# Output projection 2 of a two-block transformer kernel as seven products of quadrants

## The chip, the cores and the metric

The kernel runs on one NeuronCore (1 of 8) of a Trainium2 chip, in one launch. The metric is device microseconds of that core. The kernel before has a median of 1051.36 us over 3 runs (1051.34 to 1053.21).

Engines by their names in the profile: PE is TensorE (PEld its weight loads), DVE is VectorE, ACT is ScalarE, POOL is GpSimd, SP is SyncE, which issues most transfers.

## The reference, cut to what matters

Two transformer blocks run one after the other on 512 rows (tokens) of 1024 features, in float32. The second block's end is

```python
m = sigmoid(g_a) * y_a + sigmoid(g_b) * y_b          # 512 x 1024
h = layer_norm(ALPHA * h + m @ w_out_2, ln1_g, ln1_b)  # output projection 2, w_out_2 is 1024 x 1024
f = square(relu(h @ w_ff1)) @ w_ff2                    # 1024 -> 4096 -> 1024
h = layer_norm(ALPHA * h + f, ln2_g, ln2_b)
```

The change touches `m @ w_out_2` and the first 512 columns of `h @ w_ff1`.

## The kernel before, in words

**Numbers in two halves.** TensorE multiplies rounded float32 values. To keep accuracy each operand is split: ScalarE copies it rounded (`hi`), VectorE subtracts that copy from the original (`lo`), and TensorE makes three matmuls for each product of tiles: hi x hi, hi x lo, lo x hi (`three`, L624 to L626). So each weight block (128 x 2048) costs ScalarE one rounding copy and VectorE one subtraction, and each activation operand as well. Helper `lower` (L1861) is the subtraction of all of them.

**Blocks in order.** `block_list` lists the weight blocks. SyncE loads block n into one of two raw tiles, after VectorE has finished the low half of block n - 2. The engines each walk the same list; all instructions are written out by hand in a fixed order for each engine, and each engine takes its own strictly in that order. Semaphores (`wait_ge`, `then_inc`) tie the engines.

**Around the change.** The last four blocks before output projection 2 are those of `g_b`: TensorE makes gates in banks 0 and 1, ScalarE applies the sigmoid in the bank, VectorE multiplies (`r_silu<-r_silu,bank`, L2645) and adds the two branches (`add_branches`, `r_silu<-r_silu,u_gelu`, L2392). Each addition raises `m_ready`; at 8 all of m is there, in tile R (`r_silu`).

**Output projection 2 before.** Four blocks of w_out_2 (two halves of the columns, two halves of the inner dimension), each against the matching half of m, split in `x_hi`, `x_lo`: 4 blocks x 4 row tiles x 4 chunks x 3 = 192 matmuls of 512 columns, in banks 2 to 5. The last two blocks are interleaved (`tm_pair`, L738), so that row tile 0 is done first and the layer norm starts before the projection ends. VectorE adds each bank to the residual (`add_half`, L2545: 8 instructions), takes row statistics (L2396, L2399), centres (L2572) and, once GpSimd has made the reciprocal root (L3004, L3005), scales (L2581). TensorE transposes the four rows of h (`turn_row`, L779, 8 transposes of 128 x 128 each): rows 0 and 1 inside the projection, rows 2 and 3 inside what follows. ScalarE copies the transposed row (`act_t_hi`), and VectorE makes its low half (`h1_rows_lo`).

**The feed-forward pair.** The first two ff1 blocks run together (`ff1_pair_by_halves`): first both blocks for rows 0 and 1, 96 matmuls of 256 columns, then both for rows 2 and 3, 96 more. The first matmul waits for the low half of h's row 1 and for block 0's low half. GpSimd makes that one (`split_own`, L3007); VectorE makes block 1's (`w_ff_block_lo`). Then the rest of ff1 begins: products P1, P5, P6 and so on of a seven-product scheme; the second of them, P5, waits until VectorE has made the sums of h and their low halves, the last of which is `act_t_lo<-h_t,act_t_hi` of 128 x 1024.

**What is done by seven products already.** v and o projections of both blocks, output projection 1, ff1 after its first pair, and ff2. They make sums of weight quadrants by transfers that add to what is in the tile (`accum_op=ALU.add`), issued by GpSimd.

## Time and profile before

| what | value |
|---|---|
| median of 3 runs | 1051.36 us (1051.34, 1051.36, 1053.21) |
| the profiled execution | span 1049.6 us from its first to its last instruction, 13915 instructions |
| median less that span | 1.8 us, which lies around the first and last instruction |
| TensorE busy | 1040.1 us, 99% of the span |
| VectorE busy | 802.4 us, 76% |
| ScalarE busy | 542.5 us, 52% |
| GpSimd busy | 95.2 us, 9% |
| granted TensorE clock | 0.998 of full speed (2.4 GHz) over the span |
| transfers | 139.88 MB, mean 133 GB/s |

Busy time tells how full an engine is on average; which engine sets the pace in one stage is read from who waits there. "Idle before it" in a timeline is time in which an engine had nothing to do since the wait of the instruction behind was not yet met; "<-" names who ended the wait. Durations of a pipelined engine overlap, so the distance from one start to the next is what an instruction costs its engine when it never waits.

### The profile page before, as it was taken

The page shows a single profiled execution, that of the slowest core. Times are in us where ns is not written, and L with a number is a line of the kernel's source. Part 1 is how long each engine was busy: PE and PEld are TensorE (multiplying, and loading weights), DVE is VectorE, ACT ScalarE, POOL GpSimd, SP SyncE. Part 2 cuts the span into 40 slices and gives each one's busy share as a digit, 9 for nine tenths or more (in the row PEclk, how much of TensorE's full clock was granted, in tenths as well). Part 3 has the DMA queues.
Part 4 walks back from the last instruction along what each step waited for, and adds up shares of the span by engine and source line. Part 5 has one row for each costly group of instructions (what it writes and reads, how often), then busy time and mean ns, then how long its engine had stood idle before and what let it go on. Part 6 is the DMA issues. An engine that isn't in the chain of part 4 may idle for free.

```text
span 1049.6 us, 13915 instructions
## 1 busy us (share of the span) xinstructions
PE 1040.1 (99%) x5668; PEld 903.1 (86%) x5668; DVE 802.4 (76%) x915; ACT 542.5 (52%) x632; POOL 95.2 (9%) x108
## 2 busy tenths in 40 slices
PE   9999999999999999999999999999999999999997
PEld 8788888888888888888888888889999999888885
DVE  5778878678966787877877544678887776897897
ACT  7576653464544644355445533443556656655560
POOL 1301000000112010001101000023000000220200
PEclk9999999999999999999999999999999999999999
DMA  9847322323973665323323312361222433999962
GB/s 324 241 114 163 96 80 81 91 81 114 234 153 113 206 122 160 119 81 101 92 71 121 115 45 81 121 228 54 80 82 81 130 112 124 188 206 244 186 215 80
DMA packets 96064, 139.88 MB, mean 133 GB/s; under 512 B 5149, under 2 KB 59805, under 8 KB 95873
## 3 DMA queue, kind: packets, MB, share of 16 engines
q1 hardware_dynamic: 77808, 97.43, 28.2%
q0 software_dynamic: 17904, 41.43, 19.3%
q8 instruction: 45, 0.74, 0.3%
q10 hardware_dynamic: 288, 0.13, 0.1%
q14 instruction: 19, 0.15, 0.0%
HBM read 134.25 MB, written 4.73 MB: 132 GB/s over the span
## 4 chain that ended last, share of the span: by engine, by line
PE 98%; DMA 1%; DVE 0%; SPq 0%; ACT 0%; DVEq 0%; issue 0%
PE bank L624 31%; PE bank L625 31%; PE bank L626 31%; PE bank L779 2%; PE bank L974 1%; PE bank L898 1%; PE bank L1023 1%; DMA w_raw<-in_w_mem_kv 1%; PE bank L998 0%; PE bank L830 0%; PE bank L831 0%; DVE residual L2917 0%; DVE w_lo L1861 0%; ACT w_hi L1711 0%; PE bank L953 0%; SPq L3132 0%
## 5 line engine op out<-in xcount | busy, mean ns | idle before, releaser
L1861 DVE TENSOR_TENSOR w_lo<-w_raw,w_hi 128x2048 fp32r<-128x2048 f32 (+2 forms) x81 | 174.6, 2158 | 90.6 <-ACT w_hi L1274 70.4
L624 PE MATMUL bank<-act_t_hi,w_hi 128*128 128x512 f32 (+1 forms) x592 | 225.8, 381 | 0.0
L626 PE MATMUL bank<-act_t_hi,w_lo 128*128 128x512 f32 (+1 forms) x592 | 223.8, 378 | 0.0
L625 PE MATMUL bank<-act_t_lo,w_hi 128*128 128x512 f32 (+1 forms) x592 | 223.6, 378 | 0.0
L626 PEld LDWEIGHTS bank<-act_t_hi,w_lo 128*128 128x128 f32 x592 | 111.4, 188 | 20.9
L625 PEld LDWEIGHTS bank<-act_t_lo,w_hi 128*128 128x128 f32 x592 | 111.5, 188 | 20.0
L624 PEld LDWEIGHTS bank<-act_t_hi,w_hi 128*128 128x128 f32 x592 | 111.4, 188 | 20.0
L1274 ACT ACTIVATE w_hi<-w_raw 128x2048 fp32r<-128x2048 f32 (+1 forms) x48 | 88.9, 1855 | 29.4 <-PE bank L626 29.4
L624 PE MATMUL bank<-w_hi,hidden_hi 128*128 128x512 f32 x216 | 84.1, 389 | 0.0
L625 PE MATMUL bank<-w_lo,hidden_hi 128*128 128x512 f32 x216 | 84.0, 389 | 0.0
L626 PE MATMUL bank<-w_hi,hidden_lo 128*128 128x512 f32 x216 | 84.0, 389 | 0.0
L1861 DVE TENSOR_TENSOR w_ff_lo<-w_raw,w_ff_hi 128x1024 fp32r<-128x1024 f32 x49 | 59.6, 1222 | 28.7 <-ACT w_ff_hi L1540 28.7
L1540 ACT ACTIVATE w_ff_hi<-w_raw 128x1024 fp32r<-128x1024 f32 x49 | 51.7, 1054 | 42.9 <-DVE w_raw L2594 20.8
L1762 ACT ACTIVATE w_hi<-w_raw 128x2048 fp32r<-128x2048 f32 x28 | 53.5, 1911 | 28.1 <-DMA w_raw<-in_w_ff 24.4
L624 PE MATMUL bank<-act_t_hi,w_ff_hi 128*128 128x256 f32 x224 | 63.4, 283 | 0.0
L625 PE MATMUL bank<-act_t_lo,w_ff_hi 128*128 128x256 f32 x224 | 63.4, 283 | 0.0
L626 PE MATMUL bank<-act_t_hi,w_ff_lo 128*128 128x256 f32 x224 | 63.4, 283 | 0.0
L624 PEld LDWEIGHTS bank<-w_hi,hidden_hi 128*128 128x128 f32 x216 | 40.5, 188 | 8.6 <-DVE w_lo L1861 0.2
L626 PEld LDWEIGHTS bank<-w_hi,hidden_lo 128*128 128x128 f32 x216 | 40.5, 188 | 8.5
L625 PEld LDWEIGHTS bank<-w_lo,hidden_hi 128*128 128x128 f32 x216 | 40.5, 188 | 8.2
L624 PE MATMUL bank<-h_sum_hi,w_ff_hi 128*128 128x256 f32 x168 | 47.5, 283 | 0.0
L625 PE MATMUL bank<-h_sum_lo,w_ff_hi 128*128 128x256 f32 x168 | 47.5, 283 | 0.0
(448 smaller groups left out, 2334.0 us busy)
## 6 DMA issues: line engine op xcount, KB each, us to landing
w_raw<-in_w_in SPq DMA_DIRECT2D x38, 1024.0 KB, 5.3
w_raw<-in_w_ff POOLq DMA_DIRECT2D x16, 1024.0 KB, 14.8
w_raw<-in_w_ff SPq DMA_DIRECT2D x28, 512.0 KB, 4.9
w_raw<-in_w_ff SPq DMA_DIRECT2D x13, 1024.0 KB, 7.4
w_vo_sums<-in_w_in POOLq DMA_DIRECT2D x8, 1024.0 KB, 9.0
w_raw<-in_w_out SPq DMA_DIRECT2D x8, 1024.0 KB, 5.2
w_vo_sums<-in_w_in SPq DMA_DIRECT2D x6, 1024.0 KB, 5.3
w_out_sums<-in_w_out POOLq DMA_DIRECT2D x4, 1024.0 KB, 9.5
```

Source lines behind the costliest of these rows:

```text
L624: pe.matmul(dst, lh, rh, start=start, stop=False, skip_group_check=onto)
L625: pe.matmul(dst, lh, rl, start=False, stop=False, skip_group_check=onto)
L626: return pe.matmul(dst, ll, rh, start=False, stop=stop, skip_group_check=onto)
L779: last = pe.transpose(dst[:, tile_of(i)], src(i), IDENT[:, :])
L898: last = pe.matmul(dst[:, c:c + P + 1], PP[h % 2][:, w:w + P], V[:, i, h, :], start=i == 0, stop=i == j)
L974: last = pe.matmul(dst[:, tile_of(i)], KEP[:, c:c + P], QEC[:, c:c + P], start=True, stop=True)
L1023: last = pe.matmul(dst[:, tile_of(j)], VH[:, j, tile_of(g)], WST[:, g, :], start=True, stop=True)
L1274: act.activation(WH[slot_of(n)][:, c0:w], raw_of(n)[:, c0:w], ACT.Copy).then_inc(w_hi, 1)
L1540: act.activation(UPH[g % FF1_SLOTS][:, :, :], up_place(i), ACT.Copy).then_inc(up_hi, 1)
L1762: act.activation(MH[split_slot(p)][:, :], MRAW[s][:, :], ACT.Copy).then_inc(w_hi, 1)
L1861: return dve.tensor_tensor(dst, src, hi.bitcast(f32), ALU.subtract)
```

## The change

**The products.** m (rows halved: m index 0 is rows 0 to 255; inner dimension halved) and w_out_2 (inner dimension and columns halved) become 2 x 2 quadrants. Seven products of quadrants stand for the eight: each is 2 row tiles x 4 chunks x 3 matmuls of 512 columns. TensorE takes them in the order P1, P2, P5, P6, P3, P7, P4 (`w_out2_products`). P6, P3, P7 and P4 are accumulated on top of what an earlier product left in its bank ("chained banks"): P6 on P1 (banks 2, 3), P3 on P5 (4, 5), P7 on P6, P4 on P7 (2, 3). Each chained product first waits, tile by tile, until VectorE has added the bank's state so far to (or subtracted it from) a quadrant of the residual (`vo_added`). That makes 14 bank additions of 128 x 512 (`wo2_part_fold`, `wo2_last_fold`) where there were 8.

**The operands.** Right operands are four weight quadrants' sums: P1, P3 and P2 take a quadrant as loaded, P5, P6, P4 and P7 take a sum that a transfer made by adding a quadrant to the raw tile after the previous low half was made: three sums follow each other in one raw tile (P1, then P5, then P6, then P4). Left operands are quadrants of m or sums of them; VectorE makes four sums (`wo2_m_sum`). Each left operand (128 x 1024) is rounded by ScalarE and lowered by VectorE: 7 of them, where there were 4 of 128 x 2048.

**Feed-forward block 0.** Its low half (128 x 2048) moves from GpSimd to VectorE, which makes it after centring row 0.

**Order of ScalarE and of the loads.** After the rounded left operand of P2, ScalarE makes the weight copy of P7 before the left operand of P5 (`w_out2_operands`), and ff1's two blocks come last. SyncE loads three quadrants once the second block's last attention output is in its bank, then ff1 block 0 after P2's low half, and block 1 after P5's product (before, block 1 was loaded ahead of the projection).

```diff
+        wo2_w = a["w_out_2"][0].rearrange("(k c p) (n f) -> k n p c f", p=P, k=2, n=2)
+        WO2_RIGHT = (P1, P3, P5, P2, P7, P6, P4)
+        WO2_LEFT = (P1, P2, P5, P6, P3, P7, P4)
+        WO2_SLOT = {P1: 0, P5: 1, P3: 2, P2: 3, P7: 4, P6: 0, P4: 3}
...
+            def wo2_product(i, between=None):
+                wh, wl = (four_chunks(t) for t in wo2_right(i))
+                lh, ll = wo2_left(i)
+                pe.wait_ge(vo_lo, WO2_SPLITS + WO2_RIGHT.index(i) + 1)
+                pe.wait_ge(x_lo, E_WO2 + WO2_LEFT.index(i) + 1)
+                b0 = {P1: 2, P6: 2, P7: 2, P4: 2, P5: 4, P3: 4, P2: 6}[i]
+                onto = {P6: 0, P3: 2, P7: 4, P4: 6}.get(i)
+                for t in range(2):
+                    key = ("wo2", b0, t)
+                    if onto is None:
+                        take(b0 + t, key)
+                    else:
+                        pe.wait_ge(vo_added, WO2_ADDS + onto + t + 1)
+                    for kk in range(4):
+                        last = three(bank[b0 + t][:, :], lh[:, kk, tile_of(t)], ll[:, kk, tile_of(t)], wh[:, kk, :], wl[:, kk, :],
+                                     onto is None and kk == 0, kk == 3, onto is not None)
+                    if i in WO2_PART:
+                        last.then_inc(vo_first, 1)
+                    else:
+                        give(last, key)
+                    if between and t == 0:
+                        between()
+                if i in WO2_PART:
+                    wo2_done[i] = (vo_first, WO2_PARTS + WO2_PART[i] + 2)
+                else:
+                    b, u = turn[key]
+                    wo2_done[i] = (bank_full[b], u + 1)
+            def w_out2_products():
+                for i in (P1, P2, P5, P6, P3, P7):
+                    wo2_product(i)
+                wo2_product(P4, lambda: turn_row("h1T", h1_done, 0))
+                turn_row("h1T", h1_done, 1)
...
-            ff1_pair_by_halves({(0, 0, 5): 2, (1, 0, 3): 3})
...
+            def w_out2_operands():
+                wo2_left_hi_of(P2)
+                wo2_right_hi(P7)
+                wo2_left_hi_of(P5)
+                wo2_right_hi(P6)
+                wo2_left_hi_of(P6)
+                wo2_left_hi_of(P3)
+                wo2_left_hi_of(P7)
+                wo2_left_hi_of(P4)
+                wo2_right_hi(P4)
+                act.wait_ge(*wo2_done[P6])
+                split(ff1_0)
...
-            def center_rows(n0, j, g, v):
-                add_half(n0, 1, ALPHA, j)
+            def center_rows(j, g, v):
+                half_stats(RES, j, 0)
                 link(half_stats(RES, j, 1))
...
+            def wo2_m_sum(i):
+                if i == P5:
+                    dve.wait_ge(m_ready, KC)
+                    dve.wait_ge(*block_done[ff1_0 - 1])
+                    ins = dve.tensor_tensor(OSUM[:, :, :], m_quadrant(1, 0), m_quadrant(1, 1), ALU.subtract)
+                if i == P6: ins = dve.tensor_tensor(OSUM[:, :, :], OSUM[:, :, :], m_quadrant(0, 0), ALU.subtract)
+                if i == P3:
+                    dve.wait_ge(vo_sum, WO2_SUMS + 2)
+                    ins = dve.tensor_tensor(m_quadrant(0, 1), m_quadrant(0, 1), OSUM[:, :, :], ALU.add)
+                if i == P7: ins = dve.tensor_tensor(m_quadrant(0, 0), m_quadrant(0, 0), m_quadrant(1, 0), ALU.subtract)
+                ins.then_inc(vo_sum, 1)
+            def wo2_rows(m, n, t):
...
+            def wo2_part_fold(i, t):
+                r = wo2_rows(*{P1: (0, 0), P5: (1, 1), P6: (0, 1), P7: (1, 1)}[i], t)
+                dve.wait_ge(vo_first, WO2_PARTS + WO2_PART[i] + t + 1)
+                b = bank[(4 if i == P5 else 2) + t]
+                if i == P7:
+                    dve.wait_ge(vo_added, WO2_ADDS + WO2_PART[P5] + t + 1)
+                    ins = dve.tensor_tensor(r, r, b[:, :], ALU.subtract)
+                else:
+                    ins = dve.scalar_tensor_tensor(r, r, ALPHA, b[:, :], ALU.mult, ALU.subtract if i == P6 else ALU.add)
+                ins.then_inc(vo_added, 1)
+            def wo2_last_fold(i, t):
+                key = ("wo2", {P2: 6, P3: 4, P4: 2}[i], t)
+                r = wo2_rows(*{P2: (0, 0), P3: (0, 1), P4: (1, 0)}[i], t)
+                b = full(dve, key)
+                if i != P4:
+                    dve.wait_ge(vo_added, WO2_ADDS + WO2_PART[P1 if i == P2 else P6] + t + 1)
+                    ins = dve.tensor_tensor(r, r, b[:, :], ALU.add)
+                else:
+                    ins = dve.scalar_tensor_tensor(r, r, ALPHA, b[:, :], ALU.mult, ALU.add)
+                free(ins, key)
+                drained(dve, key)
+            def w_out2_operands():
+                wo2_m_sum(P5)
+                wo2_left_lo_of(P2)
+                wo2_left_lo_of(P5)
+                wo2_m_sum(P6)
+                wo2_right_lo(P7)
+                wo2_right_lo(P6)
+                wo2_left_lo_of(P6)
+                dve.wait_ge(x1_back, 16)
+                for t in range(2): wo2_part_fold(P1, t)
+                wo2_m_sum(P3)
+                wo2_part_fold(P5, 0)
+                wo2_left_lo_of(P3)
+                wo2_part_fold(P5, 1)
+                wo2_m_sum(P7)
+                for t in range(2): wo2_last_fold(P2, t)
+                wo2_left_lo_of(P7)
+                wo2_left_lo_of(P4)
+                wo2_right_lo(P4)
+                for t in range(2): wo2_part_fold(P6, t)
+                dve.wait_ge(ln_in, 32)
+                r0 = MT + TT + H + 3 * TT
+                wo2_last_fold(P3, 0)
+                center_rows(0, L1G, TT)
+                dve.wait_ge(w_hi, ff1_0 + 1)
+                lower(WL[2][:, :], RAW[0][:, :], WH[2][:, :]).then_inc(own_lo, 1)
+                wo2_last_fold(P3, 1)
+                wo2_part_fold(P7, 0)
+                scale_rows(0, r0, L1B, 0, h1_done)
+                center_rows(1, L1G, TT)
+                wo2_part_fold(P7, 1)
+                scale_rows(1, r0, L1B, 0, h1_done)
+                h1_rows_lo(0)
+                dve.wait_ge(w2_hi, 1)
+                lower(W2L[:, :], W2[:, :], W2H[:, :]).then_inc(w2_lo, 1)
+                wo2_last_fold(P4, 0)
+                center_rows(2, L1G, TT)
+                h1_rows_lo(1)
+                scale_rows(2, r0, L1B, 0, h1_done)
+                wo2_last_fold(P4, 1)
+                center_rows(3, L1G, TT)
+                scale_rows(3, r0, L1B, 0, h1_done)
+                h1_rows_lo(2)
+                up_lo_of(0)
+                h1_rows_lo(3)
             def wo_left_lo(x):
...
-            def split_own(n):
-                pool.wait_ge(w_hi, n + 1)
-                pool.tensor_tensor(WL[2][:, :], RAW[n % 2][:, :], WH[2][:, :].bitcast(f32), ALU.subtract).then_inc(own_lo, 1)
...
+            def add_w_out2(r, k, n, after):
+                pool.wait_ge(vo_lo, WO2_SPLITS + WO2_RIGHT.index(after) + 1)
+                pool.dma_start(four_chunks(ORAW[r]), wo2_w[k, n], accum_op=ALU.add).then_inc(quad_sum[WO2_QUEUE[r]], 16)
+            add_w_out2(0, 0, 1, P1)
+            add_w_out2(1, 0, 1, P3)
+            add_w_out2(0, 1, 1, P5)
             pool.wait_ge(m_ready, KC)
             pool.dma_start(RES[:, :, :], x1_spill.rearrange("(j p) n -> p j n", p=P)).then_inc(x1_back, 16)
             load_all(L1G[:, :], a["ln1_g_2"][0], ln_in)
             load_all(L1B[:, :], a["ln1_b_2"][0], ln_in)
-            split_own(ff1_0)
...
+                full(sp, ("o2", TT - 1, i))
+            sp.dma_start(four_chunks(ORAW[0]), wo2_w[0, 0]).then_inc(quad_raw[WO2_QUEUE[0]], 16)
+            sp.dma_start(four_chunks(ORAW[1]), wo2_w[1, 1]).then_inc(quad_raw[WO2_QUEUE[1]], 16)
+            sp.wait_ge(w_lo, ff1_0 - 1)
+            sp.dma_start(four_chunks(ORAW[2]), wo2_w[1, 0]).then_inc(quad_raw[WO2_QUEUE[2]], 16)
+            sp.wait_ge(vo_lo, WO2_SPLITS + WO2_RIGHT.index(P2) + 1)
             load(ff1_0, blocks[ff1_0][2])
+            sp.wait_ge(*wo2_done[P5])
+            sp.dma_start(W2[:, :].rearrange("p (k c) -> p k c", k=KC),
+                         a["w_ff1_2"][0].rearrange("(k p) n -> p k n", p=P)[:, :, 256:512]).then_inc(w2_loaded, 16)
```

The order of the instructions shows two places. First VectorE from the end of m to the first bank addition; `x_lo` and `m_left_lo` are low halves of left operands, `w_lo` of weights, `m_sum` sums of m's quadrants. Before:

```order
L2392 TENSOR_TENSOR r_silu<-r_silu,u_gelu 128x512 [waits bank_free0,bank_free7,bank_free6]
L2392 TENSOR_TENSOR r_silu<-r_silu,u_gelu 128x512 [waits bank_free1]
L1861 TENSOR_TENSOR w_lo_54<-w_raw_50,w_hi_52 128x2048 [waits w_hi_done]
L1861 TENSOR_TENSOR x_lo_86<-r_silu,x_hi_84 128x2048 [waits x_hi_done]
L1861 TENSOR_TENSOR w_ff_block_lo<-w_ff_block_215,w_ff_block_hi 128x2048 [waits w_ff1_block1_hi]
L1861 TENSOR_TENSOR w_lo_53<-w_raw_49,w_hi_51 128x2048 [waits w_hi_done]
L1861 TENSOR_TENSOR x_lo_85<-r_silu,x_hi_83 128x2048 [waits x_hi_done]
L1861 TENSOR_TENSOR x_lo_90<-r_silu,x_hi_88 128x2048 [waits x_hi_done]
L2545 SCALAR_TENSOR_TENSOR residual<-residual,bank 128x512 [waits bank_full2,x1_back]
```

And with the change:

```order
L2430 TENSOR_TENSOR r_silu<-r_silu,u_gelu 128x512 [waits bank_free1,bank_free7,bank_free6]
L2694 TENSOR_TENSOR m_sum<-r_silu 128x1024 [waits bank_full1,m_ready]
L1909 TENSOR_TENSOR m_left_lo<-r_silu,m_left_hi 128x1024 [waits x_hi_done]
L1909 TENSOR_TENSOR m_left_lo<-m_sum,m_left_hi 128x1024 [waits x_hi_done]
L2695 TENSOR_TENSOR m_sum<-m_sum,r_silu 128x1024
L1909 TENSOR_TENSOR w_lo_54<-w_out_sums_208,w_hi_52 128x2048 [waits w_vo_hi]
L1909 TENSOR_TENSOR w_lo_84<-w_out_sums_207,w_hi_83 128x2048 [waits w_vo_hi]
L1909 TENSOR_TENSOR m_left_lo<-m_sum,m_left_hi 128x1024 [waits x_hi_done]
L2714 SCALAR_TENSOR_TENSOR residual<-residual,bank 128x512 [waits vo_first_product,x1_back]
L2714 SCALAR_TENSOR_TENSOR residual<-residual,bank 128x512 [waits vo_first_product]
L2698 TENSOR_TENSOR r_silu<-r_silu,m_sum 128x4x256 [waits x_t_sums]
L2714 SCALAR_TENSOR_TENSOR residual<-residual,bank 128x512 [waits vo_first_product]
```

Before, six subtractions of 128 x 2048 stand between the last addition of a branch and the first bank. Now seven instructions stand there, two of 128 x 2048 and five of 128 x 1024, and another sum and four more low halves follow among the bank additions. `w_ff_block_lo` has left this place.

Second, VectorE from scaling row 1 of h to the low half of row 1, on which the feed-forward pair's first matmul waits (`act_t_lo` are the low halves of h's rows, `bn` and `mean_var` the row statistics). Before:

```order
L2581 SCALAR_TENSOR_TENSOR residual<-residual,rstd,ln_b_all 128x1024 [waits rstd_done,ln_centered]
L1861 TENSOR_TENSOR act_t_lo<-h_t,act_t_hi 128x4x128 [waits bank_free6,h1_t_hi]
L1861 TENSOR_TENSOR act_t_lo<-h_t,act_t_hi 128x4x128 [waits bank_free7,h1_t_hi]
L2545 SCALAR_TENSOR_TENSOR residual<-residual,bank 128x512 [waits bank_full4]
L2396 BN_STATS bn<-residual 128x6 [waits bank_free4]
L2399 BN_AGGR mean_var<-bn 128x2 [waits dve_chain]
L2572 SCALAR_TENSOR_TENSOR residual<-residual,mean_var,ln_g_all 128x1024 [waits ln_var]
L1861 TENSOR_TENSOR act_t_lo<-h_t,act_t_hi 128x4x128 [waits bank_free6,h1_t_hi]
L1861 TENSOR_TENSOR act_t_lo<-h_t,act_t_hi 128x4x128 [waits bank_free7,h1_t_hi]
L2581 SCALAR_TENSOR_TENSOR residual<-residual,rstd,ln_b_all 128x1024 [waits rstd_done,ln_centered]
```

And with the change:

```order
L2611 SCALAR_TENSOR_TENSOR residual<-residual,rstd,ln_b_all 128x1024 [waits rstd_done,ln_centered]
L1909 TENSOR_TENSOR act_t_lo<-h_t,act_t_hi 128x4x128 [waits bank_free6,h1_t_hi]
L1909 TENSOR_TENSOR act_t_lo<-h_t,act_t_hi 128x4x128 [waits bank_free7,h1_t_hi]
L1909 TENSOR_TENSOR w_ff_block_lo<-w_ff_block_226,w_ff_block_hi 128x2048 [waits w_ff1_block1_hi]
L2726 SCALAR_TENSOR_TENSOR residual<-residual,bank 128x512 [waits bank_full2]
L2434 BN_STATS bn<-residual 128x6 [waits bank_free2]
L2434 BN_STATS bn<-residual 128x6
L2437 BN_AGGR mean_var<-bn 128x2 [waits dve_chain]
L2602 SCALAR_TENSOR_TENSOR residual<-residual,mean_var,ln_g_all 128x1024 [waits ln_var]
L1909 TENSOR_TENSOR act_t_lo<-h_t,act_t_hi 128x4x128 [waits bank_free6,h1_t_hi]
L1909 TENSOR_TENSOR act_t_lo<-h_t,act_t_hi 128x4x128 [waits bank_free7,h1_t_hi]
L2611 SCALAR_TENSOR_TENSOR residual<-residual,rstd,ln_b_all 128x1024 [waits rstd_done,ln_centered]
```

The low half of ff1's block 1 (`w_ff_block_lo`) and a second row statistic now stand between the low halves of rows 0 and 1. TensorE has 24 instructions fewer in all (5188 rows against 5212).

## Rows read from the trace of the kernel before

**Rows 1.** Page, parts 1 and 4: busy time by engine; the chain that ended last

```profile
PE 1040.1 (99%) x5668; PEld 903.1 (86%) x5668; DVE 802.4 (76%) x915; ACT 542.5 (52%) x632; POOL 95.2 (9%) x108
...
PE 98%; DMA 1%; DVE 0%; SPq 0%; ACT 0%; DVEq 0%; issue 0%
```

**Rows 2.** Windows of output projection 2 and of the pair's first half; header names the columns

```profile
core 0: us, PE busy (x) PEld busy (x) DVE busy (x) ACT busy (x) POOL busy (x), PEclk, DMA share, GB/s
678.60:723.94 45.34, 45.34 (x209) 37.62 (x208) 35.79 (x36) 19.61 (x17) 12.74 (x10) 1.00 0.53 185
723.94:737.18 13.24, 13.24 (x113) 13.23 (x112) 11.70 (x15) 6.35 (x10) 1.85 (x3) 1.00 0.01 1
```

**Rows 3.** Output projection 2's matmuls by tile: count, duration ns, first and last start

```profile
L624 PE MATMUL bank<-w_hi,x_hi x64: 389/389/477, 678.6 to 723.3; 128*128 128x512 f32 x64
```

**Rows 4.** Timeline of TensorE: start us, us, instruction; eight transposes, then P5's first

```profile
713.96 1.06 PE L779 MATMUL bank<-ident,residual 128*128 128x128 f32 x8
714.78 0.48 PE L624 MATMUL bank<-w_hi,x_hi 128*128 128x512 f32 x1
...
751.58 0.28 PE L624 MATMUL bank<-act_t_hi,w_ff_hi 128*128 128x256 f32 x1
```

**Rows 5.** VectorE's groups, 678.4 to 724.2 us: count, busy us, mean ns, idle before

```profile
L1861 DVE TENSOR_TENSOR w_lo<-w_raw,w_hi 128x2048 fp32r<-128x2048 f32 x3 | 6.9, 2292 | 5.0 <-ACT w_hi L1274 5.0
L1861 DVE TENSOR_TENSOR x_lo<-r_silu,x_hi 128x2048 fp32r<-128x2048 f32 x3 | 6.8, 2284 | 0.0
L2545 DVE SCALAR_TENSOR_TENSOR residual<-residual,bank 128x512 f32<-128x512 f32 x7 | 4.8, 685 | 1.7 <-PE bank L626 1.7
...
L2581 DVE SCALAR_TENSOR_TENSOR residual<-residual,rstd,ln_b_all 128x1024 f32<-128x1024 f32 x3 | 3.9, 1284 | 1.6 <-POOL rstd L3005 1.6
```

**Rows 6.** Timeline of VectorE. In brackets: idle before it, and who released it

```profile
679.50 0.69 DVE L2645 TENSOR_TENSOR r_silu<-r_silu,bank 128x512 f32<-128x512 f32 x1 [1.58 <-ACT bank L1599]
680.10 1.29 DVE L2392 TENSOR_TENSOR r_silu<-r_silu,u_gelu 128x512 f32<-128x512 f32 x2
...
698.30 2.13 DVE L2545 SCALAR_TENSOR_TENSOR residual<-residual,bank 128x512 f32<-128x512 f32 x3
...
709.52 0.69 DVE L2396 BATCH_NORM_STATS2 bn<-residual 128x6 f32<-128x512 f32 x1
...
710.49 1.28 DVE L2572 SCALAR_TENSOR_TENSOR residual<-residual,mean_var,ln_g_all 128x1024 f32<-128x1024 f32 x1
...
717.56 1.28 DVE L2581 SCALAR_TENSOR_TENSOR residual<-residual,rstd,ln_b_all 128x1024 f32<-128x1024 f32 x1 [0.80 <-POOL rstd L3005]
...
722.86 1.29 DVE L1861 TENSOR_TENSOR act_t_lo<-h_t,act_t_hi 128x512 fp32r<-128x512 f32 x2
...
733.26 1.29 DVE L1861 TENSOR_TENSOR act_t_lo<-bank,act_t_hi 128x512 fp32r<-128x512 f32 x2 [0.61 <-ACT act_t_hi L1611]
...
745.33 2.35 DVE L1861 TENSOR_TENSOR h_sum_lo<-h_t,h_sum_hi 128x1024 fp32r<-128x1024 f32 x2
...
750.00 1.23 DVE L1861 TENSOR_TENSOR act_t_lo<-h_t,act_t_hi 128x1024 fp32r<-128x1024 f32 x1
```

**Rows 7.** Timeline of ScalarE: rounding copies of 1024 and 2048 elements

```profile
306.99 1.06 ACT L1637 ACTIVATE y_left_hi<-y 128x1024 fp32r<-128x1024 f32 x1 [2.51 <-PE bank L626]
307.96 1.90 ACT L1644 ACTIVATE w_hi<-w_out_sums 128x2048 fp32r<-128x2048 f32 x1
```

**Rows 8.** Timeline of GpSimd: its low half; start of one reciprocal root

```profile
704.43 4.98 POOL L3010 TENSOR_TENSOR w_lo<-w_raw,w_hi 128x2048 fp32r<-128x2048 f32 x1 [20.69 <-ACT w_hi L1274]
...
715.53 1.28 POOL L3004 TENSOR_SCALAR rstd_tmp<-mean_var 128x1 f32<-128x1 f32 x1 [3.06 <-DVE mean_var L2399]
```

**Rows 9.** Transfers of the kernel: queue, count, KB each, median us to landing

```profile
w_out_sums<-in_w_out SPq DMA_DIRECT2D x2, 1024.0 KB, 8.6
...
residual<-x_spill POOLq DMA_DIRECT2D x1, 2048.0 KB, 11.0
```

**Rows 10.** By tile w_out_sums, four adding and two plain loads: landing

```profile
DMA to landing us min/median/max: 7.2/9.5/12.5
```

247 lines of the change are left out of this document (100 added, 147 removed).

## Prediction, made before the changed kernel ran

> **What bounds the kernel now.** I read the page first, then the stretch that changes by windows, then both engines' order in it. The page: TensorE is busy 99% of the span and the chain that ended last runs through it for 98% [rows 1]. So 1 us of TensorE's work taken away is worth 1 us, as long as nobody else becomes later than it. The windows: output projection 2 takes 45.34 us, from 678.60 to 723.94, all of it TensorE, at clock 1.00; VectorE is busy 35.79 of these, so it has some 9.5 us to spare and no more [rows 2]. That is the number to keep in mind, since the change gives TensorE less to do and VectorE more. Where VectorE's spare time lies is in its groups: 5.0 us waiting for rounded weights, 1.7 for banks, 1.6 for reciprocal roots [rows 5].
>
> **TensorE's part.** One kind of matmul, 64 of the 192, spans 678.6 to 723.3 [rows 3]. The 192 and two groups of eight transposes, 0.82 us each from start to start [rows 4], fill 45.34 us: (45.34 - 1.64)/192 = 0.2276 us a matmul. Seven products instead of eight leave out 24: 24 x 0.2276 = 5.5 us. TensorE alone would start the feed-forward pair at 723.94 - 5.5 = 718.5.
>
> **VectorE's part.** The pair's first matmul waits for the first quarter-row of row 1's low half. Before, it starts at 723.94, while VectorE began that low half at 722.86 [rows 6]: about 0.4 us of slack. So the change can gain only if VectorE gets there earlier too, and I add up what it must do before that point.
>
> The start is fixed by TensorE: the last gate product is at 679.50 and takes 0.61 to the next start, one branch addition (0.61) then completes m, near 680.7 [rows 6]. (The other addition of the last block moves into the gap before that gate, whose idle time is 1.58 us.)
>
> Prices from start to start: two 1024 subtractions take 2.35 together where one takes 1.22, so one costs 1.13 and the overlap is 0.09 [rows 6]. By that overlap a 2048 low half of 2.29 costs 2.20 [rows 5], an addition from a bank 0.61, and 0.72 where VectorE also waits for its own release (three in 2.13) [rows 6]; centring and scaling 1.20 [rows 5, 6]; statistics of a row, from one half's start to centring 0.97, with a second half 1.58 [rows 6]; a row's low half in two parts, 1.29, costs 1.20 [rows 6].
>
> What stands between the end of m and the low half of row 1 now:
> ten operations of 128 x 1024 (4 sums of m, low halves of the left operands of P2, P5, P6, P3, P7, P4), 11.3; five low halves of 2048 (weights of P7, P6, P4, and both ff1 blocks), 11.0; eight additions at 0.61 and five at 0.72, 8.5; statistics, 3 x 1.58 = 4.7; three centrings and two scalings, 6.0; row 0's low half, 1.2. Sum 42.7 us.
>
> To this come waits. (a) ScalarE rounds P2's left operand after m is ready, then P7's weights, then P5's left operand. With 0.97 for a copy of 1024, 1.90 for one of 2048 and 1.06 for the last to end [rows 7], P5's copy ends at about 684.75, while VectorE is free at 683.0: 1.8 us. (b) P3's left copy follows the sum it copies: VectorE fits one bank addition into it and waits 0.6. (c) P4's weights are the fourth copy in a row on ScalarE: 0.3. (d) Row 1's reciprocal root: GpSimd began one at 715.53, VectorE scaled at 717.56 [rows 6, 8], 2.0 us in which centring and one addition fit: 0.2. Together 2.9 us.
>
> 680.7 + 42.7 + 2.9 = 726.4, and the first part of the low half ends 0.7 later: the pair starts at 727.1, against 723.94. That is **3.2 us later**, although TensorE has 5.5 us less to do; it would idle about 8.7 us, in pieces: P7 waits for P6's additions (0.2), P4's first tile for P7's (2.2: the addition stands behind centring row 0 and the ff1 low half), P4's second tile for the other of them (1.0), and the rest, 5.3 us, ahead of the pair.
>
> The same from the other side: VectorE's new work is 4 sums, 5 to 6 more bank additions and the 2.20 of ff1's block 0, some 10 us. The old waits of 8.3 us are nearly used up and 2.9 new ones come: 10 - 8 + 3 = 5, near the first sum's 3 to 4 on VectorE's side.
>
> **The moved low half.** GpSimd took 4.98 us for it [rows 8], off everyone's path. On VectorE it is 2.20 on the path. Had it stayed, the loss would be near 1 us.
>
> **What is costed at nothing.** In the `g_b` blocks VectorE and ScalarE get four weight splits early, and P1's left operand; they lie in gaps (before, those blocks held splits of w_out_2 as well). If the sum for P5 lands late, the gates queued behind P5's copy on ScalarE and VectorE wait, and m ends late: 0 to 3.0 us, the distance from 9.5 to 12.5 in landings [rows 10]; I take 0. Two plain loads issued together took 8.6 [rows 9] against 7.2 for the fastest of that tile [rows 10]; the first gate behind P1's copy can slip as well, under 1 us, and I take 0. The residual's load, issued when m is ready, takes 11.0 [rows 9]: 691.8, needed at 692.5; 0 to 0.8. Nobody else waits on GpSimd's queue behind the three additions, except that same load.
>
> P4's weights are the dangerous sum. Its transfer starts after P6's low half (691.5) and lands 7.2, 9.5 or 12.5 later [rows 10]: 698.7, 701.0, 704.0; ScalarE comes to it at 701.1. So 0, 0 or 2.9 us. I take 0 and keep 2.9. Behind that copy are VectorE's low half and all bank additions, and TensorE's P7 behind these.
> The Trainium skill (DMA: Bandwidth & Descriptors, the section on the anatomy of a GpSimd-issued DMA) gives 2.0 us plus bytes over 436e3 for such a transfer; for 1 MiB that is 4.4 us, an estimate from that page. By it the sum would land at 695.9 and could never be late; the trace's adding transfers take 7.2 at least [rows 10], and the measured ones decide. The forecast is the same by either, only the late rival would lose its chance by the page.
>
> **After the pair's start.** The first half lasts 13.24 us [rows 2]. Rows 2 and 3 of h are later by as much as row 1, so the shift stays. Later P5 of ff1 started at 751.58 [rows 4], when the low half that it needs, begun at 750.00, ended at 751.23 [rows 6]. VectorE's distance from row 3's low half (733.26 + 1.29) to there is 16.7; row 3 now ends near 737.9, so 754.6, and TensorE comes there at 751.58 + 3.2 = 754.8. No second loss, and none of the 3.2 comes back, as TensorE is full from there on [rows 1].
>
> The span would be 1049.6 + 3.2 = 1052.8. The median is 1.8 us above the profiled span, around it, and moves with it: 1051.36 + 3.2 = **1054.6 us**.
>
> **Rivals.**
> *TensorE stays the bound (faster).* The one mechanism: VectorE's chain is short enough that the pair starts by TensorE's count. In favour: five stretches already run by seven products, and TensorE is still 99% busy [rows 1]. Against: here a layer norm and the low half of h follow at once. It needs VectorE at row 1's low half by 717.8, 8.7 us earlier than my sum; any gain at all needs 3.2 us less than 45.6, 7%. Full price: 1051.36 - 5.5 = 1045.9 us; partly, up to 1049.
> *Near a tie.* The four waits vanish (ScalarE is quicker to start, or its copies are hidden otherwise). Then 3.2 - 2.9 = 0.3: 1051.7; with half of them 1053.1. Against it: the order on ScalarE is fixed, and copies of the trace are stable.
> *Late transfers (slower still).* P4's sum at 12.5 us: +2.9; the one for P5 at 12.5: up to +3.0; residual +0.8. One of the large ones: 1057.5; both: 1060.5. For: the worst landings did occur beside other loads, and here the residual and the norms' rows precede P4's sum in the same queue. Against: median 9.5.
> That the change would not do what it says is excluded: the order shows 24 matmuls fewer.
>
> **Chances.** VectorE's chain as summed, 1053.5 to 1056.0: 0.61. Late transfers, above 1056: 0.17. Near a tie: 0.13. TensorE bound: 0.09. What a measurement can tell here is 0.2%, 2.1 us. So slower 0.77 (chain nearly whole, and late), same 0.14, faster 0.09. The range 1052.0 to 1058.6 leaves out the faster case and the doubly late one. The slower cases' own range is 1053.5 to 1058.6.
>
> **What will show it.** Right: TensorE idle in the profile after, which has almost none now, ended by VectorE: before P4's two tiles by `residual` additions, and some 5.3 us ahead of the first `act_t_hi,w_hi` matmul by `act_t_lo`; VectorE without a wait over 0.7 us from about 685 to 727; that first matmul at about 727, and the matmuls of the projection starting at 678.6 as now. Wrong: no idle time ahead of the pair (then VectorE's prices are too high); P1 later than 678.6 (then the early part was not hidden); VectorE waiting on ScalarE for P4's weights by over 1 us (late transfers); or P5 of ff1 later by more than the pair (then the lag grows behind it).

## The result, and the profile after

| | before | after |
|---|---|---|
| median of 5 runs | 1051.59 us (1051.34 to 1053.21) | 1056.78 us (1056.33 to 1057.87) |
| ratio, 95% interval | | 1.0048 (1.0036 to 1.006) |
| span of the profiled execution | 1049.6 us | 1054.8 us |
| granted clock over the span | 0.998 | 0.997 |

The kernel got slower, by 5.2 us. Forecast were 1054.6 us and a range of 1052.0 to 1058.6. Here is the page first, parts 1 and 4, to lay beside [rows 1]:

```profile
PE 1038.5 (98%) x5644; PEld 900.9 (85%) x5644; DVE 818.8 (78%) x932; ACT 547.3 (52%) x638; POOL 96.5 (9%) x111
...
PE 94%; DVE 3%; ACT 1%; DMA 1%; issue 1%; DVEq 0%; POOL 0%; POOLq 0%
```

TensorE has 24 instructions fewer, but its busy time fell by 1.6 us only, and the last chain now leaves it for 6% of the span, half of that for VectorE. The waits of TensorE from 679 to 728 us (total, how often, longest) say where; before there was none in this stretch [rows 2]:

```profile
PE bank L648 <- DVE act_t_lo L1909: 5.1, 1, 5.1
PE bank L648 <- DVE residual L2712: 2.5, 2, 1.9
PE bank L648 <- DVE residual L2714: 0.2, 1, 0.2
```

The windows of the projection and of the pair's first half, which answer to [rows 2], and inside the latter a piece at another clock (columns as there; the last but two is the granted clock):

```profile
679.08:727.76 48.68, 40.89 (x186) 33.02 (x184) 44.83 (x48) 19.97 (x20) 10.70 (x10) 1.00 0.56 173
727.76:741.94 14.18, 14.18 (x109) 14.18 (x110) 12.41 (x15) 6.33 (x10) 2.09 (x3) 0.90 0.01 1
...
727.76:730.00 2.24, 2.24 (x10) 2.24 (x11) 2.24 (x3) 0.00 (x0) 0.26 (x1) 0.50 0.04 7
730.00:733.44 3.44, 3.44 (x29) 3.44 (x28) 2.78 (x5) 0.00 (x0) 1.70 (x2) 0.90 0.00 0
```

VectorE is busy for 44.83 of 48.68 us, where it was for 35.79 of 45.34. That is the stage's new bound.
```profile
727.76 0.55 PE L648 MATMUL bank<-act_t_hi,w_hi 128*128 128x256 f32 x1 [5.15 <-DVE act_t_lo L1909]
728.11 0.41 PE L649 MATMUL bank<-act_t_lo,w_hi 128*128 128x256 f32 x1
728.32 0.41 PE L650 MATMUL bank<-act_t_hi,w_lo 128*128 128x256 f32 x1
```

VectorE's timeline at the points that the prediction named (answers to [rows 6]): the first sum of m, P5's left operand, P4's weights, block 0's low half, the scaling of row 1, block 1's low half, row 1's low half, and the last operand that P5 of ff1 needs:

```profile
681.52 1.23 DVE L2694 TENSOR_TENSOR m_sum<-r_silu 128x1024 f32<-128x1024 f32 x1
...
685.37 1.23 DVE L1909 TENSOR_TENSOR m_left_lo<-m_sum,m_left_hi 128x1024 fp32r<-128x1024 f32 x1 [1.48 <-ACT m_left_hi L1649]
...
703.59 2.29 DVE L1909 TENSOR_TENSOR w_lo<-w_out_sums,w_hi 128x2048 fp32r<-128x2048 f32 x1 [0.18 <-ACT w_hi L1638]
...
710.48 2.29 DVE L1909 TENSOR_TENSOR w_lo<-w_raw,w_hi 128x2048 fp32r<-128x2048 f32 x1
...
718.84 1.28 DVE L2611 SCALAR_TENSOR_TENSOR residual<-residual,rstd,ln_b_all 128x1024 f32<-128x1024 f32 x1 [0.20 <-POOL rstd L3099]
...
721.24 2.29 DVE L1909 TENSOR_TENSOR w_ff_block_lo<-w_ff_block,w_ff_block_hi 128x2048 fp32r<-128x2048 f32 x1
...
726.92 1.29 DVE L1909 TENSOR_TENSOR act_t_lo<-h_t,act_t_hi 128x512 fp32r<-128x512 f32 x2
...
755.17 1.23 DVE L1909 TENSOR_TENSOR act_t_lo<-h_t,act_t_hi 128x1024 fp32r<-128x1024 f32 x1
```

**Where the 5.2 us are.** Four points of a trace split the span: P1's first matmul, the pair's first, the first with `w_ff_hi`, the end.

| kernel | P1 starts | stage, to the pair | idle ahead of the pair | pair | rest | span |
|---|---|---|---|---|---|---|
| before | 678.60 | 45.34 | 0 | 24.76 | 300.9 | 1049.6 |
| after | 679.08 | 48.68 | 5.15 | 26.12 | 300.9 | 1054.8 |
| difference | 0.5 | 3.3 | 5.15 | 1.4 | 0.0 | 5.2 |

Of the first 0.5 us, 0.4 are there at 36 us, where both programs do the same; over all 14 traces of this study P1 starts between 678.38 and 679.76, median 679.08, and experiment 4, an edit of the kernel before, has 679.07. It is scatter, and the profiled execution of before was an early one (its later medians are 1051.7 to 1051.9). The 3.3 and the 1.4 belong to the change. A single time carries this scatter of some 1 us, so small effects are read below from the stage, the pair and the rest of a trace, and the medians stand beside them.

### The profile page after: what moved, and what is told of

Read it like the earlier page. It is cut to its first block, busy times and chain, and to the rows that moved or that the text cites. A ratio compares the mean times of both kernels' runs of the same rounds, so it can differ in the third digit from the quotient of the medians.

```text
span 1054.8 us, 13902 instructions
## 1 busy us (share of the span) xinstructions
PE 1038.5 (98%) x5644; PEld 900.9 (85%) x5644; DVE 818.8 (78%) x932; ACT 547.3 (52%) x638; POOL 96.5 (9%) x111
## 4 chain that ended last, share of the span: by engine, by line
PE 94%; DVE 3%; ACT 1%; DMA 1%; issue 1%; DVEq 0%; POOL 0%; POOLq 0%
PE bank L648 29%; PE bank L650 29%; PE bank L649 29%; PE bank L769 2%; DVE w_lo L1909 1%; PE bank L964 1%; PE bank L888 1%; DMA w_raw<-in_w_in 1%; PE bank L1013 1%; PE bank L777 1%; PE bank L988 0%; PE bank L821 0%; PE bank L820 0%; ACT w_hi L1638 0%; ACT m_left_hi L1649 0%
## 5 line engine op out<-in xcount | busy, mean ns | idle before, releaser
L1909 DVE TENSOR_TENSOR w_lo<-w_raw,w_hi 128x2048 fp32r<-128x2048 f32 (+2 forms) x79 | 170.1, 2155 | 86.7 <-ACT w_hi L1296 65.2
L1296 ACT ACTIVATE w_hi<-w_raw 128x2048 fp32r<-128x2048 f32 (+1 forms) x44 | 81.4, 1849 | 19.4 <-PE bank L650 19.4
L1559 ACT ACTIVATE w_ff_hi<-w_raw 128x1024 fp32r<-128x1024 f32 x49 | 51.6, 1054 | 42.9 <-DVE w_raw L2624 20.8
```

Source lines behind the costliest of these rows:

```text
L1296: act.activation(WH[slot_of(n)][:, c0:w], raw_of(n)[:, c0:w], ACT.Copy).then_inc(w_hi, 1)
L1559: act.activation(UPH[g % FF1_SLOTS][:, :, :], up_place(i), ACT.Copy).then_inc(up_hi, 1)
L1909: return dve.tensor_tensor(dst, src, hi.bitcast(f32), ALU.subtract)
```

## The experiments

Each kernel was timed in 5 to 11 runs beside the kernel before (medians 1051.7 to 1051.9; the changed kernel's own ratio is to 1051.59). All but the fourth are edits of the changed kernel. The last four columns come from one profiled execution each: the stage from P1 to the pair, the idle time ahead of the pair (a part of the stage), the pair, and the rest.

| experiment | time, us | ratio to before, 95% | stage | idle | pair | rest |
|---|---|---|---|---|---|---|
| changed kernel | 1056.78 | 1.0048 (1.0036 to 1.006) | 48.68 | 5.15 | 26.12 | 300.9 |
| 1 low half of block 0 on GpSimd | 1055.83 | 1.0038 (1.0025 to 1.0052) | 47.34 | 5.19 | 26.32 | 300.9 |
| 2 matmuls in the wait | 1055.82 | 1.0037 (1.0023 to 1.0051) | 48.94 | 0.65 | 24.83 | 300.9 |
| 3 ScalarE's order | 1056.89 | 1.0047 (1.0033 to 1.006) | 47.15 | 5.19 | 26.30 | 300.9 |
| 4 before, block 0 on VectorE | 1053.59 | 1.0018 (1.0009 to 1.0027) | 47.26 | 0 | 24.76 | 300.9 |
| 5 without adding transfers | 1057.43 | 1.005 (1.0036 to 1.0064) | 49.48 | 5.25 | 26.65 | 300.8 |
| 6 both low halves on GpSimd | 1057.87 | 1.0058 (1.0045 to 1.0072) | 49.69 | 4.29 | 26.30 | 300.9 |
| 7 as 6, with 3 | 1056.12 | 1.0041 (1.0028 to 1.0055) | 47.89 | 4.28 | 26.26 | 300.9 |
| 8 block 1's low half later | 1058.32 | 1.0063 (1.0049 to 1.0077) | 47.27 | 3.07 | 28.11 | 305.0 |
| 9 edits 1, 2 and 3 | 1052.57 | 1.0008 (0.9999 to 1.0017) | 45.87 | 0.59 | 24.82 | 301.0 |
| 10 as 9, block 1 later | 1053.55 | 1.0015 (1.0005 to 1.0024) | 43.65 | 0.64 | 24.83 | 304.6 |
| 11 block 1 later, with matmuls | 1055.89 | 1.0038 (1.0025 to 1.0052) | 46.46 | 0.64 | 24.83 | 303.1 |
| 12 VectorE relieved | 1050.18 | 0.9987 (0.9978 to 0.9996) | 42.64 | 2.62 | 26.31 | 300.9 |

### 1. Block 0's low half back on GpSimd

```diff
-                lower(WL[2][:, :], RAW[0][:, :], WH[2][:, :]).then_inc(own_lo, 1)
+            # on GpSimd, ahead of the reciprocal roots
+            pool.tensor_tensor(WL[2][:, :], RAW[0][:, :], WH[2][:, :].bitcast(f32), ALU.subtract).then_inc(own_lo, 1)
```

> The changed kernel, with the low half of the first feed-forward block made by GpSimd again, ahead of its four reciprocal roots. Theory (VectorE's chain sets the pair's start, and TensorE's own idle time ahead of it brings slow matmuls): VectorE is 2.2 us shorter, of which GpSimd's late reciprocal root for row 0 takes back 0.4 to 1.1; the pair starts at 725.9 to 726.7 instead of 727.8, after an idle time of 3.3 to 4.1 us in place of 5.15. Time 1055.3 if the matmuls behind it are still slow for as long, 1053.9 if they are not. Rival A (late transfers set the stage's end): 1056.8, no change. Rival B (the loss lies in TensorE's seven products themselves): 1056.8.

The pair starts at 726.63, inside the forecast, and the time is 1055.83 where 1055.3 was forecast. The stage is 1.3 us shorter, not 2.2. VectorE's and GpSimd's timelines show where the rest went (VectorE's row first):

```profile
709.45 2.18 DVE L2602 SCALAR_TENSOR_TENSOR residual<-residual,mean_var,ln_g_all 128x1024 f32<-128x1024 f32 x1
```
```profile
705.62 4.92 POOL L3193 TENSOR_TENSOR w_lo<-w_raw,w_hi 128x2048 fp32r<-128x2048 f32 x1 [11.58 <-ACT w_hi L1296]
```

The centring of row 0, 1.28 us elsewhere, takes 2.18 and ends 1.1 us after GpSimd's subtraction does (710.54): it was held up by it. So the part of the change that moved this low half to VectorE cost the stage 1.3 us. The idle time ahead of the pair did not shrink, against the expectation. TensorE's transposes of row 1 came earlier by the same amount, so that idle time is a distance on VectorE, from row 1's scaling to its low half, and not what is left over from TensorE's shorter work.

### 2. Matmuls in TensorE's wait

```diff
+                                if b == 0 and t == 0:
+                                    for _ in range(20):
+                                        pe.matmul(bank[0][:, :], wh[:, 0, tile_of(0)], WH[2][:, 0:512], start=True, stop=True, ...)
```

> The changed kernel, with 20 matmuls of 128x512 on operands that lie ready, into a bank that the pair then starts anew, between the second row's transposes and the first matmul of the feed-forward pair (about 4.5 us in the wait of 5.15). Theory: the pair starts at 727.8 as before, VectorE's chain being the same, but the granted clock stays at 1.0 behind it, so that its first 36 matmuls take 4.3 us instead of 5.7: time 1055.4, 1.4 under the changed kernel. Rival (the slow start of the pair comes from its operands or from VectorE's and ScalarE's work beside it, not from the idle time): the same 5.7 us for these matmuls, 1056.8.

The same two pieces as above, by windows: the wait, now filled, and the start of the pair.

```profile
722.77:727.95 5.18, 4.54 (x20) 3.44 (x20) 5.08 (x8) 1.66 (x4) 1.89 (x2) 1.00 0.00 0
727.95:730.19 2.24, 2.24 (x19) 2.24 (x20) 2.24 (x3) 0.00 (x0) 0.27 (x1) 1.00 0.00 0
```

19 matmuls start in 2.24 us instead of 10, at clock 1.00, with VectorE and ScalarE doing the same beside them. The pair is back at 24.83 us, 1.3 less. So the slow start is a matter of the idle time ahead of it, not of operands. The Trainium skill (TensorE: Matmul & The Clock Gate, section "What's actually happening") says that the engine's clock is halved when it has been idle and comes back after sustained work; this trace agrees, with 0.50 behind the wait and 1.00 without one. The median fell by 1.0 us, and the intervals of the two ratios overlap, so the time alone would not show it; the trace does. Three of the five timed runs have a mean clock of 0.996, the other two 0.998 and 0.999: this edit fills only the last wait, and the waits ahead of P4, 2.4 us in sum, are still there.

### 3. ScalarE's order

```diff
                 wo2_left_hi_of(P2)
+                wo2_left_hi_of(P5)
                 wo2_right_hi(P7)
-                wo2_left_hi_of(P5)
                 wo2_right_hi(P6)
```

> The changed kernel, with ScalarE copying the left operand of M1 to M7's P5 ahead of P7's right one, so that VectorE's wait of 1.48 us at 685 goes. Theory: the whole chain of VectorE behind it moves up by 1.1 to 1.5 us, the pair starts at 726.3 to 726.7, TensorE waits 3.7 to 4.1 us, and the slow matmuls stay: time 1055.3 to 1055.7. Rival (TensorE's products or transfers set the end, VectorE's wait is covered): 1056.8, the pair still at 727.8.

The wait of 1.48 us is gone and the stage is 1.5 us shorter, as the theory has it. The median, 1056.89, is the rival's number (1056.8) and not the forecast one, so here time and trace speak against each other. Two things bear on it: P1 started 0.7 us late in the profiled execution (1055.89 us), and three of the other four had a mean clock of 0.994 in place of 0.997; the latter is the likely cause, not shown, as only one execution has a trace. 0.003 of 1054 us, at half the rate, is some 6 us more at the low clock, part of it spent in waits. So other falls of the clock than the one ahead of the pair occur in some executions; experiment 5 shows one.

### 4. The kernel before, with block 0's low half on VectorE

```diff
                         center_rows(n - 1, j, L1G, TT)
+                        if j == 0:
+                            dve.wait_ge(w_hi, ff1_0 + 1)
+                            lower(WL[2][:, :], RAW[0][:, :], WH[2][:, :]).then_inc(own_lo, 1)
                         scale_rows(j, r0, L1B, 0, h1_done)
...
-            split_own(ff1_0)
```

> The kernel before, with the one part of the change alone: VectorE instead of GpSimd makes the low half of the first feed-forward block, between centring and scaling of row 0. Its 2.2 us stand in place of a wait for the reciprocal root of 0.8, so that VectorE's last chain (row 1's low half, which ends at 724.1) is 1.4 later. Theory: TensorE, which did not wait there, waits 0.8 to 1.5 us for row 1's low half: 1052.7 to 1053.4 beside 1051.9 for the kernel before. If GpSimd's reciprocal root of row 0 had been late by its long low half, that comes back and it is 0.3 less. Rival (VectorE has the room there, this part costs nothing): 1051.9.

1.8 us slower, stage 1.9 longer; the forecast was 0.8 to 1.5. GpSimd's timeline has what was missed:

```profile
711.01 1.28 POOL L3007 TENSOR_SCALAR rstd_tmp<-mean_var 128x1 f32<-128x1 f32 x1 [26.81 <-DVE mean_var L2399]
712.37 2.50 POOL L3008 TENSOR_TENSOR rstd<-rstd_tmp,minus_half 128x1 f32<-128x1 f32 x1
```

A reciprocal root of one column takes 2.50 us instead of 0.57. It began 0.22 us behind VectorE's subtraction of 2.28 us and ended 0.4 us after it, so VectorE waited another 0.54 us for it ahead of scaling row 0; the forecast's 1.4 us on VectorE and these 0.54 make the 1.9. TensorE waited too, but at another place than forecast: 1.73 us ahead of a row's transposes, for a scaling, and not ahead of the pair. The changed kernel has the same root of 2.50 us, without harm, since two bank additions stand behind the subtraction there. Before, the low half stood on GpSimd while VectorE waited for banks, added them and took statistics, so it cost nobody anything.

### 5. No adding transfers

```diff
-            add_w_out2(0, 0, 1, P1)
-            add_w_out2(1, 0, 1, P3)
-            add_w_out2(0, 1, 1, P5)
...
-            add_w_out2(0, 1, 0, P6)
```

> The changed kernel without the four adding transfers for the second output projection's weights: the products P5, P6, P4 and P7 take the quadrant that lies there, unsummed. Theory (VectorE's chain): the same, 1056.8, at most 0.3 less through the 0.18 us wait for P4's copy. Rival (the transfers are late or slow the others down): the waits shrink and the time falls by 1 us or more, to 1055.8 or less.

This kernel leaves out the sums of quadrants and the waits for them; ScalarE then waits for the plain loads alone. Nothing is gained, so the rival of late transfers falls: in the changed kernel ScalarE comes to P4's sum at 701.64 and VectorE waits 0.18 for that copy, and here it is 0.16. The time is 1057.43 where 1056.8 was forecast. The stage is even 0.8 longer. TensorE's timeline in P4's first tile:

```profile
714.25 0.47 PE L648 MATMUL bank<-w_hi,m_left_hi 128*128 128x512 f32 x1 [1.91 <-DVE residual L2709]
...
715.47 0.44 PE L650 MATMUL bank<-w_hi,m_left_lo 128*128 128x512 f32 x1
715.71 0.63 PE L648 MATMUL bank<-w_hi,m_left_hi 128*128 128x512 f32 x1
716.14 0.63 PE L649 MATMUL bank<-w_lo,m_left_hi 128*128 128x512 f32 x1
```

The window 716.00 to 718.27 has clock 0.50. In the changed kernel's profile the same wait, 1.89 us, was followed by no such fall. The same wait thus costs its length in one execution and 0.8 us more in another; which, these runs don't tell apart.

### 6 and 7. Both low halves on GpSimd, and ScalarE's order with them

```diff
                 rstd(RST[:, j:j + 1], MV[:, j, 1:2], 1, 1.0, LN_EPS)
+                if j == 1:
+                    pool.wait_ge(w2_hi, 1)
+                    pool.tensor_tensor(W2L[:, :], W2[:, :], W2H[:, :].bitcast(f32), ALU.subtract).then_inc(w2_lo, 1)
```

> The changed kernel, with the low halves of both feed-forward blocks made by GpSimd: the first ahead of the reciprocal roots as in the run with that alone (1055.8), the second between the root of row 1 and that of row 2. Theory: as the second low half (2.3 us) stands between the last scaling and row 1's low half on VectorE, TensorE's idle time ahead of the pair, 5.2 us in all four runs so far, falls to 2.9, and the pair starts at about 724.3. Time 1053.5 if the matmuls behind the wait are still slow, 1052.2 if 2.9 us of idle time no longer do that. Rival (GpSimd's long operation slows VectorE or makes the root of row 2 late, as it did for row 0 by 1 us): 1054.5 or more.

> As the kernel with both low halves on GpSimd, with ScalarE's copy of P5's left operand ahead of P7's right one besides. Theory: another 1.0 to 1.5 us less, since the whole chain of VectorE starts its long part earlier: the pair at about 723.0, time 1052.2 with slow matmuls behind the wait and 1050.9 without. Rival (GpSimd's low half of the first block, which cannot start before ScalarE's copy at 705.3, makes the root of row 0 late and sets the chain): no gain over the kernel without this.

The forecast of 1053.5 for the first missed by 4.4 us, on the side of its rival, and that of 1052.2 for the second by 3.9. VectorE's row, then GpSimd's:

```profile
717.39 5.53 DVE L2611 SCALAR_TENSOR_TENSOR residual<-residual,rstd,ln_b_all 128x1024 f32<-128x1024 f32 x1 [0.20 <-POOL rstd L3095]
```
```profile
717.25 4.58 POOL L3197 TENSOR_TENSOR w_ff_block_lo<-w_ff_block,w_ff_block_hi 128x2048 fp32r<-128x2048 f32 x1
```

A scaling of 1.28 us takes 5.53: it started 0.14 us behind GpSimd's operation and ended 1.1 us after it. So 4.3 of GpSimd's 4.6 us went to the path, in place of 2.2 on VectorE. The Trainium skill (SBUF — State Buffer, section "SBUF: two separate sides") calls this an exclusive lock: a VectorE operation with two SBUF inputs and a GpSimd operation that reads SBUF exclude each other for the whole instruction, and the one that starts first keeps the other out. The traces agree in both directions, 5.53 for 1.28 here and 2.50 for 0.57 in experiment 4. Experiment 7 takes 1.8 us off the stage of 6, where ScalarE's order took 1.5 in experiment 3.

### 8. Block 1's low half later

```diff
                 scale_rows(2, r0, L1B, 0, h1_done)
+                lower(W2L[:, :], W2[:, :], W2H[:, :]).then_inc(w2_lo, 1)
...
-            ff1_pair_by_halves({(0, 1, 3): 2, (1, 0, 3): 3})
+            ff1_pair_by_halves({(0, 1, 3): 2, (1, 1, 5): 3})
```

(The same `lower` and its wait no longer stand behind `h1_rows_lo(0)`.)

> The changed kernel, with VectorE's low half of the second feed-forward block moved from ahead of row 1's low half to behind the scaling of row 2, and the transposes of row 3 moved from the 60th to the 90th product of the pair's first half. Nothing is taken off VectorE, only what it does ahead of the pair's start. Theory: the idle time ahead of the pair falls from 5.2 to 2.9 us, the pair starts 2.3 us earlier, at 725.5; the second half of the pair then waits up to 1 us for row 3's low halves. Time 1054.5 to 1055.5, and 1.3 less if 2.9 us of idle time leave the clock up. Rival (VectorE's amount of work in the stage sets the time, not its order): 1056.8.

The idle time fell to 3.07 us, forecast 2.9, but the time rose by 1.5: above the forecast and above its rival. Row 3's transposes were too late (740.99; row 3's low half waited 3.71 us), P5 of ff1 waited 2.5 us, and behind that wait too the clock fell. The profiled execution is the slowest of the five (1061.51 us, mean clock 0.992; the median is 1058.32), and its clock is about 0.5 in three places: behind P4's first wait, for 6.1 us at the start of the pair, and behind P5's wait. Its stage, pair and rest show how the time was lost, and not how much a usual execution loses. The edit mixed a good move with a bad one, so experiments 10 and 11 separate them.

### 9. Three edits together

The edits of experiments 1, 2 and 3.

> The changed kernel with three of the edits tried alone: the first feed-forward block's low half on GpSimd (1.1 us less), ScalarE's copy of P5's left operand ahead of P7's right one (0.9 to 1.5 less), and 20 matmuls that keep TensorE busy in its wait ahead of the pair (1.0 to 1.3 less). Theory (one chain on VectorE, and a clock that falls in TensorE's idle time behind it): the three add up, as none is covered by another: the pair at about 725.5, 1053.2 to 1053.8, still 1.5 to 2 over the kernel before. Rival (they share one cover, as where a second chain takes over): 1055 or more.

1052.57 us, ratio 1.0008 (0.9999 to 1.0017): 4.2 us under the changed kernel, and not to be told from the kernel before. The three add up, to a little less than the forecast of 1053.2 to 1053.8. TensorE's row at the pair's start:

```profile
725.02 0.36 PE L648 MATMUL bank<-act_t_hi,w_hi 128*128 128x256 f32 x1 [0.59 <-DVE act_t_lo L1912]
```

The mean clock is 0.998 or 0.999 in each of its 11 runs, where the changed kernel's lies at 0.995 to 0.997: the waits ahead of P4's two tiles, 2.5 us in sum in the changed kernel, are 0.4 here, and no fall is left.

### 10 and 11. Block 1's low half later, row 3 in time

```diff
                 center_rows(3, L1G, TT)
+                h1_rows_lo(2)
                 scale_rows(3, r0, L1B, 0, h1_done)
-                h1_rows_lo(2)
...
+            ff1_pair_by_halves({(0, 1, 3): 2, (1, 1, 2): 3})
```

(with block 1's low half as in 8, and 10 matmuls in the wait; 10 has edits 1 and 3 besides.)

> The kernel with these three, with 10 matmuls in place of 20, and the second block's low half (still VectorE's) behind the scaling of row 2, row 2's low halves ahead of the scaling of row 3, and row 3's transposes at the 80th product of the pair's first half instead of the 60th. Theory: another 2.3 us off the pair's start, to about 723.2, of which row 3's low halves at the second half's start give 0 to 1 back: 1050.9 to 1052.0, even with the kernel before (1051.8) or just under it. Rival (as in the run with the low half moved alone, row 3 comes late and takes more than is won): 1054 or more.

> The changed kernel with only the moves of the kernel with four edits (second block's low half later, row 2's low halves ahead of row 3's scaling, row 3's transposes at the 80th product) and the 10 matmuls in the wait; VectorE's work is the same as in the changed kernel. Theory: what stands on VectorE between the scaling of row 1 and row 1's low half sets TensorE's idle time: it falls from 5.2 to 2.9 us, and with the clock kept up the time is 1053.5 to 1054.5. Rival (VectorE's amount of work decides; what is put off comes back before the pair's second half): 1055.8, as with the matmuls alone.

Both forecasts missed: 1053.55 for 1050.9 to 1052.0, and 1055.89 for 1053.5 to 1054.5, where the rival had 1055.8. The cause is the same in both. The pair starts 2.2 us earlier, at 722.87 in 10 as forecast; then TensorE's timeline has, in 10 and in 11:

```profile
752.77 0.36 PE L648 MATMUL bank<-act_t_hi,w_ff_hi 128*128 128x256 f32 x1 [2.02 <-DVE act_t_lo L1912]
```
```profile
755.13 0.35 PE L648 MATMUL bank<-act_t_hi,w_ff_hi 128*128 128x256 f32 x1 [2.02 <-DVE act_t_lo L1912]
```

That is P5 of ff1, waiting for the operand which VectorE began at 755.17 in the changed kernel. The pair's own second half came in time. So what decides is VectorE's amount of work from m to that operand, not its order ahead of the pair: 11 ends at 1055.89, like experiment 2 at 1055.82. In 10's profile the clock fell once more, behind this wait (0.56 from 754.30 to 758.00), and the rest took 3.6 us longer than in 9, which is more than the 2.2 us won ahead of the pair. In 11's profile the clock stayed at 1.00 behind the same wait of 2.02 us.

### 12. VectorE relieved

```diff
-                lower(WL[2][:, :], RAW[0][:, :], WH[2][:, :]).then_inc(own_lo, 1)
+                lower(WL[2][:, 0:64], RAW[0][:, 0:64], WH[2][:, 0:64]).then_inc(own_lo, 1)
...
-                half_stats(RES, j, 0)
```

(the same for W2L; TensorE takes the high halves in their place; ScalarE's order as in 3. This kernel leaves out part of the product and of the statistics, so it is a probe of time and no candidate.)

> The changed kernel with ScalarE's copies in the other order and less VectorE work: of the low halves of both feed-forward weight blocks only 64 of 2048 columns are made (TensorE takes the high half twice instead), and the statistics of the first half of each of the four rows are left out. VectorE does 2.2 + 2.2 + 4 x 0.6 = 6.8 us less; TensorE's products, the adding transfers, the chained banks and all waits stay. Theory (VectorE's amount is what bounds the stage and the half block behind it): of the 4.4 us of low halves, the 1.9 us of statistics of rows 0 to 2 and the 0.9 to 1.5 us of the wait for the copy, less 0.5 for reciprocal roots that are now waited for, the pair's start gets all: about 720.9 instead of 727.8, and the time is 1049.9 with slow matmuls behind a wait of some 2.5 us and 1048.5 without, under the kernel before (1051.8). That would be the part of the 5.5 us of saved products that reaches the end once VectorE has room. Rival (the chained banks, the transfers or TensorE's order hold the stage at another point): 1052 or more.

1050.18 us, forecast 1049.9, ratio 0.9987 (0.9978 to 0.9996), the only one under the kernel before. The pair starts at 721.02, forecast 720.9, though helped by an early P1 (678.38): the stage is 6.0 us shorter where 6.9 were forecast. TensorE's row there, and the windows behind it:

```profile
721.02 0.36 PE L648 MATMUL bank<-act_t_hi,w_hi 128*128 128x256 f32 x1 [2.62 <-DVE act_t_lo L1909]
```
```profile
721.02:722.00 0.98, 0.98 (x8) 0.98 (x9) 0.98 (x2) 0.00 (x0) 0.26 (x1) 1.00 0.06 17
722.00:725.50 3.50, 3.50 (x19) 3.50 (x19) 3.40 (x5) 0.00 (x0) 1.17 (x1) 0.51 0.00 0
```

The clock falls here 1 us after work has begun again, behind 2.6 us of idle time, and the pair takes 26.31 us. Of 11 runs two have a mean clock of 0.999, and these took 1048.86 and 1049.38 us. Stage less idle time is 42.64 - 2.62 = 40.0 us: TensorE's seven products and two groups of transposes, which the prediction put at 45.34 - 5.5 = 39.9. TensorE has no other wait in this stage, so the chained banks and the adding transfers hold nothing up here.

## Why the prediction was right, and where it was short

**TensorE gives up 5.5 us: right.** 40.0 us of work against 39.9 (experiment 12).

**VectorE's chain sets the pair's start: right, in size too.** Summed were 42.7 us of work and 2.9 of waits, from the end of m to row 1's low half. Measured from the first sum of m at 681.52 to that low half at 726.92 are 45.4 us, forecast 45.6. (The sum's end is 726.3 and not the 726.4 written there; that changes nothing. Its start, 680.7, was 0.8 us early: 0.5 is the scatter of P1, the rest the last steps to m.) The waits were 1.48 for 1.8 (a), 0.53 for 0.6 (b), 0.18 for 0.3 (c) and 0.20 for 0.2 (d). The stage grew by 3.3 us, forecast 3.2. Experiments 1 and 3 take one term each out of the sum, experiment 12 several, and the stage follows: 1.3 of 2.2, 1.5 of 1.5, and 6.0 of 6.9. The idle time was forecast in four pieces: 0.2, 2.2, 1.0 and 5.3; measured 0.18, 1.89, 0.58 and 5.15.

**The moved low half: right in sign.** "Had it stayed, the loss would be near 1 us" is a stage of 46.3; experiment 1 had 47.3, a loss of 2.0, since the sum did not know that GpSimd and VectorE exclude each other and so took the full 2.2 for it.

**Transfers at nothing: right.** Experiment 5, and P4's copy 0.18 late. The landings, to lay beside [rows 10]:

```profile
DMA to landing us min/median/max: 5.1/8.8/13.7
```

The tile now has eight adding transfers and four plain loads, half of them of output projection 1. The longest landing, 13.7 us, lies above the 12.5 of [rows 10] and made nobody late. In the `g_b` blocks ScalarE waited 4.4 us for P1's plain load and 1.9 for P5's sum (until 665.52, while the next gate came to it at 668.40), and TensorE waited for no transfer there. None came down to the 4.4 us that the prediction worked out, as an estimate, from the Trainium skill (DMA: Bandwidth & Descriptors, the section on the anatomy of a GpSimd-issued DMA): the least is 5.1, in a view that has plain loads too.

**"After the pair's start": the step that was short.** The prediction had "No second loss" there. It took the first half's 13.24 us over from a trace in which TensorE had not waited. In truth the pair took 1.4 us more, in part at half the clock, because of the 5.3 us of idle time that the same text forecast; experiment 2 shows the cause by taking it away. Of the 2.2 us between 1054.6 and 1056.78 these are 1.4, and 0.5 are the scatter ahead of P1. The prediction's own sign for this came: "P5 of ff1 later by more than the pair". P5 is 5.2 us later than before, the pair's start 3.8. Its sign "P1 later than 678.6" came as well, by 0.5 us, and is the scatter told above. The other half of that step held: the rest is 300.9 us in both, and P5 of ff1, put at 754.8 for TensorE with the operand done at 754.6, came at 756.76 with the operand begun at 755.17 and done at 756.4. Both were later by about the same, since row 3's low half waits for TensorE's transposes. How close that was, experiments 10 and 11 show: 2.2 us of an earlier pair come back as 2.0 us of wait there.

**The range: right with some luck.** 1053.5 to 1056.0 was the span for VectorE's chain as summed, and what lies above 1056 was kept for late transfers, at 0.17. The measured 1056.78 lies there, with the chain as summed and without a late transfer: the room that it fell into had been left for another mechanism, and the slow clock had no term and no chance.

**The rivals.** TensorE as the bound (1045.9) needed VectorE 8.7 us earlier; with 6.8 us of work and a wait of 1.5 us taken away the time is still 1050.2. Near a tie: not reached by taking away the largest of the four waits (experiment 3), only with two more edits (experiment 9, 1052.57). Late transfers: not seen.

**Where the 5.5 us went.** They became idle time of TensorE, and so did the 3.3 us by which the stage grew: 48.68 - 39.9 = 8.8 us, forecast 8.7. The trace shows 7.8 of these as waits (the four pieces above). The other 1.0 it counts as busy, 40.89 us in place of 39.9: the last matmul ahead of each wait is counted to its end, and the first one behind it is 0.31 to 0.33 us from the next where 0.23 is usual. What fills the waits is VectorE's work, 44.83 us busy in the stage for 35.79 [rows 2]: 9.0 us more is the price of the seven products and of the moved low half here.

**What stays open.** Why the clock fell behind a wait of 1.9 us in experiment 5's profile and not in the changed kernel's, and behind one of 2.02 us in experiment 10's and not in 11's; what share of the timed runs had such a fall; and whether a version that takes VectorE's statistics to ScalarE would beat the kernel before. Experiment 12 took 6.8 us of work and the wait of 1.5 us off VectorE's chain, for 1.5 us.

## What to carry to other kernels

Saving matmuls pays only where the engine that prepares operands and empties banks has room in that stage, and its room is counted to the point where the next stage's operands need it, not just to the next start.
